# Three norms of a two-layer transformer kernel write upper parts column by column out of PSUM, with sums of modulations split and parts of the first attention put earlier

## The reference, cut to what matters

```python
c_act = silu(c)
for i in range(2):
    sh_a, sc_a, g_a, sh_f, sc_f, g_f = split(c_act @ ada_w[i] + ada_b[i], 6)
    h = rms_norm(x, norm_g[i, 0]) * (1.0 + sc_a) + sh_a
    y = moba_attention(h, ...) if i == 0 else diff_attention(h, ...)
    x = x + g_a * rms_norm(y, norm_g[i, 1])
    h = rms_norm(x, norm_g[i, 2]) * (1.0 + sc_f) + sh_f
    x = x + g_f * rms_norm(swiglu(h, ffn_w_in[i], ffn_w_out[i]), norm_g[i, 3])
```

## Time and profile before

| | us |
|---|---|
| median of 3 runs | 930.62 (930.31 to 931.87) |
| the profiled execution | 930.76 |
| its span | 929.0 |
| TensorE busy | 900.5 |
| VectorE busy | 691.6 |
| ScalarE busy | 513.0 |
| granted clock of TensorE, mean | 0.997 |

### The profile page before, as it was taken

One profiled execution on the slowest core, in us unless ns is written; L12 is line 12 of the kernel. 1 busy time (PEld: TensorE's weight loads), 2 busy tenths in 40 slices (PEclk: granted clock), 3 DMA queues, 4 the chain that ended last, 5 costly groups with the idle time before them and its releaser, 6 DMA issues.

```text
span 929.0 us, 14108 instructions
## 1 busy us (share of the span) xinstructions
PE 900.5 (97%) x5676; PEld 807.2 (87%) x5676; DVE 691.6 (74%) x924; ACT 513.0 (55%) x811; POOL 19.0 (2%) x64
## 2 busy tenths in 40 slices
PE   5999999999999999999999999999999999999996
PEld 3999888999999979998798888898987999999875
DVE  5979987888888778989796655556896855555565
ACT  4556647544444387777864444444893744444464
POOL 3000000000000000000000000000000000000000
PEclk9999999999999999999999999999999999999999
DMA  9999962998897927674398655572444866556511
GB/s 338 365 368 348 362 218 93 385 382 316 288 340 247 322 97 233 224 249 154 128 366 284 190 193 185 181 215 91 137 152 165 273 193 193 191 189 228 184 46 46
DMA packets 130851, 212.74 MB, mean 229 GB/s; under 512 B 7793, under 2 KB 96994, under 8 KB 130786
## 3 DMA queue, kind: packets, MB, share of 16 engines
q1 hardware_dynamic: 128896, 206.46, 65.1%
q0 software_dynamic: 1504, 5.26, 1.8%
q10 hardware_dynamic: 386, 0.12, 0.1%
HBM read 210.75 MB, written 1.06 MB: 228 GB/s over the span
## 4 chain that ended last, share of the span: by engine, by line
PE 78%; DVE 11%; ACT 6%; issue 2%; DMA 2%; ACTq 0%; DVEq 0%
PE ps L738 23%; PE ps L739 23%; PE ps L740 23%; PE ps L800 2%; DVE w_lo L1860 2%; PE ps L802 2%; DVE ada_sum L1897 2%; DVE w_lo L1853 2%; DVE ada_sum L1879 2%; DMA raw<-in_moba_w_qkv 1%; PE ps L808 1%; ACT w_hi L1325 1%; ACT w_hi L1317 1%; ACT yg L1380 1%; PE ps L1020 1%
## 5 line engine op out<-in xcount | busy, mean ns | idle before, releaser
L738 PE MATMUL ps<-h_hi,w_hi 128*128 128x256 f32 x912 | 259.3, 284 | 0.0
L740 PE MATMUL ps<-h_hi,w_lo 128*128 128x256 f32 x912 | 258.1, 283 | 0.0
L739 PE MATMUL ps<-h_lo,w_hi 128*128 128x256 f32 x912 | 258.0, 283 | 0.0
L1317 ACT ACTIVATE w_hi<-raw 128x1024 fp32r<-128x1024 f32 x139 | 146.7, 1055 | 191.1 <-PE ps L740 174.9
L1853 DVE TENSOR_TENSOR w_lo<-raw,w_hi 128x1024 fp32r<-128x1024 f32 x139 | 170.0, 1223 | 110.2 <-ACT w_hi L1317 110.1
L738 PEld LDWEIGHTS ps<-h_hi,w_hi 128*128 128x128 f32 x912 | 174.9, 192 | 1.3 <-DVE w_lo L1867 0.2
L739 PEld LDWEIGHTS ps<-h_lo,w_hi 128*128 128x128 f32 x912 | 174.9, 192 | 1.1
L740 PEld LDWEIGHTS ps<-h_hi,w_lo 128*128 128x128 f32 x912 | 174.9, 192 | 0.0
L1860 DVE TENSOR_TENSOR w_lo<-raw,w_hi 128x1024 fp32r<-128x1024 f32 x139 | 169.4, 1218 | 0.7 <-ACT w_hi L1325 0.5
L1325 ACT ACTIVATE w_hi<-raw 128x1024 fp32r<-128x1024 f32 x139 | 145.6, 1048 | 5.9 <-DMA raw<-in_w_up 2.2
L738 PE MATMUL ps<-w_hi,o_hi 128*128 128x512 f32 x264 | 105.1, 398 | 1.5 <-DVE w_lo L1860 1.1
(11 more groups left out here) (340 smaller groups left out, 1240.5 us busy)
## 6 DMA issues: line engine op xcount, KB each, us to landing
ada_raw<-in_ada_w SPq DMA_DIRECT2D x32, 1024.0 KB, 8.7
raw<-in_ffn_w_in SPq DMA_DIRECT2D x52, 512.0 KB, 5.8
raw<-in_ffn_w_out SPq DMA_DIRECT2D x44, 512.0 KB, 6.2
raw<-in_ffn_w_in SPq DMA_DIRECT2D x72, 256.0 KB, 4.0
raw<-in_w_up SPq DMA_DIRECT2D x32, 512.0 KB, 4.6
raw<-in_w_down SPq DMA_DIRECT2D x32, 512.0 KB, 4.5
raw<-in_moba_w_qkv SPq DMA_DIRECT2D x24, 512.0 KB, 10.0
raw<-in_diff_w_qkv SPq DMA_DIRECT2D x20, 512.0 KB, 4.9
```

Source lines behind the costliest of these rows:

```text
L738: T.matmul(out_ap, hi_s, hi_m, start=start, stop=False, skip_group_check=True)
L739: T.matmul(out_ap, hi_s, lo_m, start=False, stop=False, skip_group_check=True)
L740: return T.matmul(out_ap, lo_s, hi_m, start=False, stop=stop, skip_group_check=True)
L1317: A.activation(w_hi[:, n.place, FRONT], raw[:, n.raw_place, FRONT], ACT.Copy).then_inc(front_hi, 1)
```

## The change

1. In z = 1, 2, 3 ScalarE writes `h_hi` of the first unit (c=0) of each t straight out of PSUM, one 128x128 tile after the other (`hi_direct`); TensorE waits for each tile (`hi_begun`, the last `hi_ready`). VectorE computes all four tiles of this unit into `yg`: first 2 and 3 (`t_half`), then, behind ScalarE's first two, 0 and 1. ScalarE waits for `t_half` ahead of tiles 2 and 3. The second units keep their form. VectorE's order: `y_gain(1,1)` ahead of the tiles, each `low` behind its own unit.
2. `turn_second` stands behind all products of t=0.
3. The 32 records of `reduce_mods(2, (1, 2))` become two blocks of 16 in two places.
4. `exps(1)` goes behind two copies. In pair j=3 of layer 0 the keys' copy stands ahead of `split_hi` (ScalarE) and `biased` ahead of `split_lo` and `gate_lo` (VectorE).
5. `rel_loaded` becomes `rowsA_loaded` (64), and two semaphores of the end become `final_rows_loaded`.

```diff
--- before.py
+++ after.py
@@ -175,6 +175,12 @@
 
 
 WIDE = 32
+DIRECT = (1, 2, 3)
+
+
+def begun(z, t, k):
+
+    return 6 * (z - 1) + 3 * t + k + 1
 
 
 def first_unit(l, pairs):
...
@@ -503,7 +509,7 @@
             queue.dma_start(rowsA[0:ROW_C, :], ada_b.rearrange("l (t p) -> (l t) p", p=P)).then_inc(rowsA_loaded, 16)
             queue.dma_start(rowsA[ROW_C:ROW_C + KT, :], row_tiles(c[0])).then_inc(rowsA_loaded, 16)
             queue.dma_start(rowsA[ROW_SUBLN:ROWS_A, :], diff_subln_g).then_inc(rowsA_loaded, 16)
-            queue.dma_start(rel_rows[:], rel_bias).then_inc(rel_loaded, 16)
+            queue.dma_start(rel_rows[:], rel_bias).then_inc(rowsA_loaded, 16)
 
 
         def load_vectors(queue):
...
@@ -793,15 +799,21 @@
                 for t in range(ST):
                     for s in range(2):
                         wh, wl = as_halves(w_hi[:, (n + s).place]), as_halves(w_lo[:, (n + s).place])
-                        pe.wait_ge(hi_ready, 4 * z + 2 * t + s + 1)
+                        direct = z in DIRECT and s == 0
+                        if not direct:
+                            pe.wait_ge(hi_ready, 4 * z + 2 * t + s + 1)
                         for k in range(4):
                             if t == 0 and k % 2 == 0:
                                 pe.wait_ge((front_lo, slab_lo)[k // 2], n.plus(s + 1))
+                            if direct and k < 3:
+                                pe.wait_ge(hi_begun, begun(z, t, k))
+                            elif direct:
+                                pe.wait_ge(hi_ready, 4 * z + 2 * t + 1)
                             T.matmul(ps[:, banks[t]], h_hi[:, 4 * s + k, tokens(t)], wh[:, k], start=s == 0 and k == 0,
                                      stop=False, skip_group_check=True)
                             T.matmul(ps[:, banks[t]], h_hi[:, 4 * s + k, tokens(t)], wl[:, k], start=False, stop=False,
                                      skip_group_check=True)
-                        if (t, s) == (0, 1):
+                        if (t, s) == (0, 1) and z not in DIRECT:
                             turn_second()
                         pe.wait_ge(h_ready, 4 * z + 2 * t + s + 1)
                         for k in range(4):
...
@@ -811,6 +823,8 @@
                             last.then_inc(slab_done, 1)
                     if t == 0:
                         last.then_inc(first_done, 1)
+                        if z in DIRECT:
+                            turn_second()
 
             def v_slab(n, meanwhile=None):
                 pe.wait_ge(front_lo, n.plus(1))
...
@@ -873,13 +887,17 @@
                                         ones[:, 0:WIDE], start=True, stop=True)
                 last.then_inc(ada_reduced, 1)
 
-            def reduce_mods(bank, slots, first=0, wide=WIDE):
-                for s, slot in enumerate(slots):
-                    for t in range(KT):
-                        at = first + (s * KT + t) * wide
-                        last = T.matmul(ps[:, bank, at:at + wide], ada_sum[:, slot, t * P:(t + 1) * P], ones[:, 0:wide],
-                                        start=True, stop=True)
-                last.then_inc(ada_reduced, 1)
+            def reduce_mod(bank, slot, first=0, wide=WIDE):
+
+                for t in range(KT):
+                    at = first + t * wide
+                    last = T.matmul(ps[:, bank, at:at + wide], ada_sum[:, slot, t * P:(t + 1) * P], ones[:, 0:wide],
+                                    start=True, stop=True)
+                return last
+
+            def reduce_mods(bank, slot):
+
+                reduce_mod(bank, slot).then_inc(ada_reduced, 1)
 
             def spread_row(banks, b):
 
...
@@ -932,9 +950,8 @@
                 last.then_inc(tok_turned, 1)
 
             pe.wait_ge(ident_step, 2)
-            pe.wait_ge(rowsA_loaded, 48)
+            pe.wait_ge(rowsA_loaded, 64)
             T.transpose(ps[:, 0, 0:ROWS_A], rowsA[0:ROWS_A, :], ident[0:ROWS_A, 0:ROWS_A]).then_inc(tab_turned, 1)
-            pe.wait_ge(rel_loaded, 16)
             T.transpose(ps[0:HEADS, 1, 0:N_BUCKETS], rel_rows[:], ident[0:N_BUCKETS, 0:N_BUCKETS])\
                 .then_inc(rel_turned, 1)
             pe.wait_ge(const_ready, 3)
...
@@ -1085,6 +1102,16 @@
                 pe.wait_ge(o_ready, PAIRS * l + 1)
                 row_slab(n, OP_ACC[l], heads(0), True)
 
+                def later_shift():
+
+                    pe.wait_ge(ada_acc, summed(ADA_LATER - 4))
+                    reduce_mod(2, 1, 256, 16)
+
+                def later_scale():
+
+                    pe.wait_ge(ada_acc, summed(ADA_LATER))
+                    reduce_mod(2, 2, 384, 16).then_inc(ada_reduced, 1)
+
                 def last_attention(quarter):
                     if quarter == 1:
                         turn_probs(pairs, (5, 6))
...
@@ -1095,17 +1122,15 @@
 
                 pe.wait_ge(o_ready, PAIRS * l + 2)
                 row_slab(n + 1, OP_ACC[l], heads(1), False, last_attention)
-                if l:
+                if l == 0:
+                    later_shift()
+                else:
                     pe.wait_ge(ada_acc, summed(ADA_GF))
-                    reduce_mods(0, (SLOT_COLS,))
+                    reduce_mods(0, SLOT_COLS)
                 pe.wait_ge(o_ready, PAIRS * l + 3)
 
-                def later_mods():
-                    pe.wait_ge(ada_acc, summed(ADA_LATER))
-                    reduce_mods(2, (1, 2), 256, 16)
-
                 row_last_two(n + 2, OP_ACC[l], heads(2), heads(3), lambda: pe.wait_ge(o_ready, PAIRS * l + 4),
-                             (lambda: turn_heads(PAIRS)) if l else later_mods, (0, 0, 0) if l else (0, 1, 1))
+                             (lambda: turn_heads(PAIRS)) if l else later_scale, (0, 0, 0) if l else (0, 1, 1))
                 turn_first(2 * l + 1)
 
                 def spread_sums():
...
@@ -1385,9 +1410,18 @@
 
                 unit = 2 * t + c
                 t_modulated(z, unit, t, c, gains, shift)
-                act.wait_ge(t_act_ready, 4 * z - 2 + unit + 1)
+                act.wait_ge(t_act_ready, 2 * z + t + 1)
                 act.wait_ge(t_ready, T_BASE[z] + unit + 1)
                 A.activation(h_part(h_hi, t, c), turned_tile(t, c), ACT.Copy).then_inc(hi_ready, 1)
+
+            def hi_direct(z, t, gains, shift):
+
+                act.wait_ge(turned, 4 * z + 2 * t + 1)
+                for k in range(4):
+                    if k == 2:
+                        act.wait_ge(t_half, 2 * (z - 1) + t + 1)
+                    A.activation(h_hi[:, k, tokens(t)], turned_to(z, t, k), ACT.Identity, bias=mods[:, shift, k:k + 1],
+                                 scale=gains[:, k:k + 1]).then_inc(hi_begun if k < 3 else hi_ready, 1)
 
             def first_copy(pair):
 
...
@@ -1436,11 +1470,11 @@
                 y_square(b, a, banks, slab, 1, 0)
                 y_square(b, a, banks, slab, 1, 1)
                 act.wait_ge(gain_ready, gains_done)
-                modulated(z, 0, 0, gains, shift)
+                hi_direct(z, 0, gains, shift)
                 y_root(b, 1)
                 modulated(z, 0, 1, gains, shift)
                 x_squares(z, 1)
-                modulated(z, 1, 0, gains, shift)
+                hi_direct(z, 1, gains, shift)
                 modulated(z, 1, 1, gains, shift)
 
             def tokens_out(n, banks, t):
...
@@ -1546,9 +1580,9 @@
                     first_hi(5, 1)
                     first_out(2)
                     split_hi(Slab(FIRST))
-                    exps(1)
                     first_out(3)
                     first_out(4)
+                    exps(1)
                     split_hi(Slab(FIRST + 1))
                     copy_turned(1, TURNED_FIRST)
                     exps(2)
...
@@ -1571,7 +1605,7 @@
                         exps(pairs + 1)
                         split_hi(n + 5)
                         return
-                    late = l == 0 and j == 2
+                    late = l == 0
                     if not late:
                         split_hi(n + 3)
                     act.wait_ge(slab_done, n.plus(1))
...
@@ -1990,6 +2024,12 @@
             def t_modulated(z, unit, t, c, gains, shift):
 
                 dve.wait_ge(turned, 4 * z + unit + 1)
+                if c == 0:
+                    for k in range(2, 4):
+                        last = V.tensor_scalar(turned_tile(t, 0)[:, k], turned_to(z, t, k), gains[:, k:k + 1],
+                                               mods[:, shift, k:k + 1], ALU.mult, ALU.add)
+                    last.then_inc(t_half, 1)
+                    dve.wait_ge(hi_begun, begun(z, t, 1))
                 for f in range(2):
                     k = 4 * c + f
                     last = V.tensor_scalar(turned_tile(t, c)[:, f], turned_to(z, t, k), gains[:, k:k + 1],
...
@@ -2004,6 +2044,9 @@
 
             def lo_part(z, unit, t, c):
                 dve.wait_ge(hi_ready, 4 * z + unit + 1)
+                if z in DIRECT and c == 0:
```

(30 more changed lines are left out.)

## The result

| | before | after |
|---|---|---|
| median of the runs, us | 930.61 (929.73 to 931.87, 5 runs) | 934.67 (934.35 to 935.03, 5 runs) |
| ratio, 95% interval | | 1.0044, 1.0032 to 1.0056 |
| span of the profiled execution | 929.0 | 933.2 |
| TensorE busy | 900.5 | 902.1 |

The change made the kernel slower by 4.1 us, where 2.4 were forecast. In the profile after, lines have moved: L800/802/808 are L812/814/820, L738 to L740 are L744 to L746, L1390 is L1415, L902 is L920, L930 is L948 and L1020 is L1037.

The account below looks back on a forecast made before the run. TensorE, busy 900.5 of 929.0 us, was taken as the bound. Start −1.7 and norms +1.2, +1.7, +1.2 sum to +2.4, from 930.76 to 933.16; less 0.14 gives 933.0 us, range 927.8 to 935.0.

Parts of the forecast that it names:

- the waits for `h_hi`: Sign in each norm: the two waits of TensorE for ScalarE's copy, 1.50 and 0.63 us, gone or below 0.5.
- Startup: TensorE's first transpose also waits for `rel_rows`: start up to 1.47 us later, about 0.7 left after a wait at 64.29.
- The x chain: VectorE's work ahead of the first norm: scaling 1.1 us later, ending 138.35, so transposes at 138.4 instead of 140.05.
- Pair 3: Keys' copy and `biased` moved ahead in layer 0: TensorE's waits fall, between nothing and −0.9 us, taken as −0.9.
- The sums: Split modulation sums ahead of the first norm: clock stays at 1.00, −1.5 us, TensorE reaching the transposes at 138.2.
- The idle rule: Skill's claim that idle gaps of TensorE lower the clock; by it, splitting the sums would bring nothing.
- Rival 3: Clock stays low behind the sums or falls behind a block of 8: transposes at 139.7, total 934.3 us; chance 0.15.
- The norms: Direct columns win 1.0 us inside, but later queues delay the next slab or tokens: +1.2, +1.7 and +1.2 us.
- `x_update`: VectorE's step in the second norm's t=0: starts at 338.9 instead of 337.70, +1.2 us.
- the last copy of t=1: ScalarE's copy in each norm, with the table load behind it: +1.7 us, 1.0 from later transposes, 0.7 from the order.
- Rival 1: Direct columns do what they say: last copy of t=1 near 344.8, table load unmoved, total 927.9 us; chance 0.2.

Follow-up runs that it names:

- r6: The kernel before with the merged semaphore alone, so the first transpose also waits for `rel_rows`: 931.27 us, ratio 1.0017.
- r7: The changed kernel with `exps(1)` ahead of the two copies again: 934.73 us, ratio 1.0051 to the kernel before.
- r5: The changed kernel with `rel_rows` counted on a separate semaphore again, so the first transpose doesn't wait for it: 933.33 us, ratio 1.0036 to the kernel before.
- r4: The kernel before with the sums split in two blocks of 16 and the change's order of pair 3, nothing else: 927.76 us, ratio 0.9977.
- r3: The kernel before with only the 32 records split into two blocks of 16: 928.80 us, ratio 0.9990.
- r1: The changed kernel with the three norms as before; startup, pairs and split sums stay changed: 929.53 us, ratio 0.9996 to the kernel before.
- r12: The kernel before with split sums, pair 3's new order, later table load and direct columns in t=1 alone, VectorE's order as before: 926.48 us, ratio 0.9963.

## Why the prediction was right, and where its sizes were off

The direction and the range held (934.67, 0.3 below its upper end), and the mechanism did: slower, by the queue of last copy, table load, split and `w_lo`. One of the signs that I named didn't come: the waits for `h_hi` are not all below 0.5, with 0.76 at a direct tile of t=0 and 0.60 at each second unit. By its steps:

- **Startup.** I gave TensorE +0.7 at 64. Measured +0.82 (65.11 instead of 64.29). That the size fits is in part luck. I had the wait of 0.76 swallow the delay because its copies "don't move with it". They do: in r6, the merge alone, the wait is still there (0.48) and the cost is 1.4 to 1.6. In the change it is gone because `exps(1)` stands behind the copies: with `exps(1)` back (r7) it is 0.59.
- **The x chain.** This is the first term that failed. I wrote that `normalised(1)` comes 0.96 later, "up to 1.5 with the startup", and took 1.1. The two add: 1.48 (ScalarE's split at 60.38 instead of 58.90) and 0.95 make 2.43, and the scaling at z=1 came 2.42 later. I had seen that VectorE has no gap to absorb it, and then didn't add the whole. So the transposes are at 139.33 instead of 138.4: 0.9 us of the miss. It would be 1.3, had I not let them begin at the end of the scaling, 0.88 behind its start; they begin 0.54 behind it. r5 and r7 each take one part out: the scaling begins at 137.56 and 137.82.
- **Pair 3.** −0.9 expected; r4 against r3 gives −1.04.
- **The sums.** −1.5 expected, TensorE itself at 138.2; measured 139.33 − 1.04 = 138.29, and the clock at 1.00. The idle rule of the Trainium skill (TensorE: Matmul & The Clock Gate, HAM oscillation — how this bites in real kernels) doesn't account for this: the fall came with TensorE busy and went with the split. Rival 3 is out, as the clock stayed at 1.00 behind both blocks. But the −1.5 holds only against executions with the stretch of 3.4 us, as the profiled one; I took one execution for the kernel.
- **The norms.** +1.2, +1.7 and +1.2 expected, +1.43, +2.04 and +1.67 measured; +4.1 became +5.1, which r1 shows as a whole (934.67 − 929.53 = 5.14). `x_update` was right (+1.18 for +1.2). The step that failed is the last copy of t=1: +2.06 instead of +1.7. The transposes of t=1 were 1.12 later instead of 1.0, and behind them 0.94 instead of 0.7. I gave the four tiles with their crossing 1.55 and they took 1.70, because VectorE stands 0.2 for ScalarE's slower tiles twice; the last copy begins another 0.1 behind VectorE's last tile.
- **Rival 1** (direct columns do what they say) is out for the whole change, as the table load was at 12.7 and not within 11. In t=1 alone, with VectorE's old order, it comes near to that: r12.

## What to carry to other kernels

A wait of the bounding engine shows what may be won at that place at most; whether it is won is decided by the next thing it will need, here a weight slab whose slack was 0.4 us. When a step is shared out anew between two engines, write down the last instruction of each in the new order and who stands behind it: 2.3 of the 5.1 us lost here were two steps in the wrong order on an engine that wasn't the bound. And delays that meet in a queue without gaps are added, not compared. Where times come in clumps, sort the executions by their granted clock before comparing medians.
